# Gates in one narrow pass, and the first norm's gain moved into the weights on GpSimd

## The reference

```python
h = rms_norm(x, norm_mix_g)                 # x * rsqrt(mean(x*x) + eps) * norm_mix_g
proj = jnp.einsum('bsd,de->bse', h, w_in)   # 1024 x 3592
a_q, a_k, a_v, d_qkv, d_z, d_beta, d_alpha = jnp.split(proj, splits, axis=-1)
a_out = chunked_band_attention(a_q, a_k, a_v, ...)      # 8 heads of 64
d_qkv = silu(causal_depthwise_conv(d_qkv, conv_w))
o = gated_delta_rule(d_q, d_k, d_v, d_beta, d_alpha, a_log, dt_bias)   # 4 heads of 128
x = x + concat(norm(a_out), norm(o) * silu(d_z)) @ w_out
x = x + (silu(rms_norm(x, norm_ffn_g) @ w_gate) * (rms_norm(x, norm_ffn_g) @ w_up)) @ w_down
```

## Time and profile before

| | |
|---|---|
| median of three runs | 1297.86 us |
| the profiled execution | 1299.1 us |
| its span in the trace | 1297.4 us |
| PE busy | 1274.9 us (98%) |
| DVE, ACT, POOL busy | 727.2, 581.3, 709.4 us |

### The profile page before, as it was taken

One profiled execution on the slowest core, in us unless ns is written; L12 is line 12 of the kernel. 1 busy time (PEld: TensorE's weight loads), 2 busy tenths in 40 slices (PEclk: granted clock), 3 DMA queues, 4 the chain that ended last, 5 costly groups with the idle time before them and its releaser, 6 DMA issues.

```text
span 1297.4 us, 18370 instructions
## 1 busy us (share of the span) xinstructions
PE 1274.9 (98%) x6956; PEld 1070.5 (83%) x6956; DVE 727.2 (56%) x1034; ACT 581.3 (45%) x931; POOL 709.4 (55%) x486
## 2 busy tenths in 40 slices
PE   8999999999999999999999999999999999999999
PEld 7888888888888877888887888888888888888887
DVE  6455654535716667845486566656555556435552
ACT  5577744654126774552353332233333324644441
POOL 4322455633325572124257996898788784754541
PEclk9999999999999999999999999999999999999999
DMA  5611345531125013553111544432444337986663
GB/s 212 236 58 33 99 136 137 150 114 49 41 45 191 3 30 124 173 187 118 69 66 65 187 187 189 162 148 116 166 187 186 154 122 264 318 287 194 195 194 146
DMA packets 77807, 186.11 MB, mean 143 GB/s; under 512 B 20680, under 2 KB 24848, under 8 KB 70680
## 3 DMA queue, kind: packets, MB, share of 16 engines
q1 hardware_dynamic: 72144, 180.71, 40.6%
q10 hardware_dynamic: 5576, 4.23, 1.1%
HBM read 130.59 MB, written 56.94 MB: 145 GB/s over the span
## 4 chain that ended last, share of the span: by engine, by line
PE 86%; DVE 5%; ACT 3%; POOL 3%; issue 2%; DMA 1%; ACTq 0%; DVEq 0%; POOLq 0%
PE ps L2147 29%; PE ps L364 20%; PE ps L2172 16%; PE ps L377 7%; PE ps L1970 2%; PE ps L2004 2%; PE ps L1992 1%; PE ps L2064 1%; DVE SX L1755 1%; PE ps L1950 1%; PE ps L349 1%; POOL WR L802 1%; PE ps L2022 1%; POOL GR L775 1%; PE ps L2034 1%
## 5 line engine op out<-in xcount | busy, mean ns | idle before, releaser
L364 PE MATMUL ps<-HT,SPLIT 128*128 128x512 f32 (+1 forms) x1488 | 328.4, 378 | 2.5 <-DVE HT L340 2.0
L364 PEld LDWEIGHTS ps<-HT,SPLIT 128*128 128x128 f32 x1488 | 264.5, 188 | 52.5 <-DVE HT L340 2.5
L2172 PE MATMUL ps<-S,HI 128*128 128x512 f32 x616 | 189.6, 389 | 0.0
L978 POOL TENSOR_TENSOR S<-RAB,S 128x512 fp32r<-128x512 f32 x77 | 106.8, 1390 | 93.2 <-ACT S L1149 92.8
L310 POOL CAST SPLIT<-RAW 128x1024 fp32r<-128x1024 f32 x31 | 33.5, 1081 | 187.1 <-PE ps L364 182.2
L2172 PEld LDWEIGHTS ps<-S,HI 128*128 128x128 f32 x616 | 115.7, 188 | 24.1
L2147 PE MATMUL ps<-S,WR 128*128 128x512 f32 x516 | 120.5, 389 | 0.4 <-POOL WR L802 0.4
L2172 PE MATMUL ps<-S,LO 128*128 128x512 f32 x308 | 119.8, 389 | 0.0
L1637 DVE TENSOR_TENSOR LO<-RAB,HI 128x512 fp32r<-128x512 f32 x77 | 66.1, 868 | 92.8 <-ACT HI L1146 92.8
L2147 PE MATMUL ps<-HI,WR 128*128 128x512 f32 x360 | 115.0, 390 | 0.2 <-POOL WR L802 0.2
L2147 PEld LDWEIGHTS ps<-S,WR 128*128 128x128 f32 x516 | 96.8, 188 | 20.8 <-POOL WR L802 0.8
(11 more groups left out here) (278 smaller groups left out, 2489.6 us busy)
## 6 DMA issues: line engine op xcount, KB each, us to landing
hidden<-HB SPq DMA_DIRECT2D x11, 1792.0 KB, 6.6
RAB<-hidden SPq DMA_DIRECT2D x77, 256.0 KB, 3.1
RAW<-units SPq DMA_DIRECT2D x37, 512.0 KB, 4.0
RAWG<-w_gate SPq DMA_DIRECT2D x11, 1024.0 KB, 10.8
RAWU<-w_up SPq DMA_DIRECT2D x11, 1024.0 KB, 4.9
RAWD<-w_down SPq DMA_DIRECT2D x11, 1024.0 KB, 8.8
down_t<-RAWD SPq DMA_DIRECT2D x11, 1024.0 KB, 4.1
RAB<-down_t SPq DMA_DIRECT2D x44, 256.0 KB, 3.4
```

Source lines behind the costliest of these rows:

```text
L364: mm = pe.matmul(ps[:, bank + a // HALF, a % HALF:a % HALF + width], w, right[other][:, k, a:a + width], start=(k == order[0] and part == ...
L978: pool.tensor_tensor(down_b(q, 1), RAB[:, q % RAWS, 1, :], down_b(q, 0).bitcast(F32), ALU.subtract).then_inc(R["b_lo"], 1)
L2172: mm = pe.matmul(ps[:, bank + t, :], down_a(q, part)[:, t * P:(t + 1) * P], down_b(q, other), start=(p == 0 and i in (1, 6, 5, 7) and part ...
```

## The change

- The gate columns come as an array of their own, 64 floats a partition (32 KB), loaded by ACT's queue. `gate_split` on POOL multiplies them by the gain and writes both parts side by side: 16 columns of weights. `gate_columns` on PE makes all four products of parts with 16 matmuls a quarter in place of 24, of 16 output rows. ACT copies 16 rows, and the turn is now a product with `fold`, a 16 x 8 matrix of two unit matrices stacked, which adds the two halves. DVE makes `fold`.
- `units` no longer holds the padded gate unit. SP loads tile 0 behind x block 1, where the gate unit was, and nothing behind block 3.
- The gain is loaded as one column of 8 values a partition, not as 4 KB in every partition. `unit_split` multiplies each of the 28 tiles in `RAW` by it before the cast (a third POOL operation, 128 x 1024). `norm_scale` for this norm is a product with one number a row. Tile 0's split waits until blocks 0 and 1 are scaled.
- 24 transposes at the start in place of 48.
- On DVE: the copy in `EXT` moves behind block 1; `side_split(dve, 0, 0)` moves ahead of the gates' arithmetic; tile 21's copy stands after step 17 of the solve in place of step 20.

```diff
-WARM, WARM_NEXT = 48, 16
+WARM, WARM_NEXT = 24, 16
+NGATE = 2 * NHD
...
         def unit_dma(sp, j, slot):
-            sp.dma_start(RAW[:, slot, :], units[j, :, :]).then_inc(raw_in[slot], 16)
+            sp.dma_start(RAW[:, slot, :], units[j - U_TILE, :, :]).then_inc(raw_in[slot], 16)
...
             pool.wait_ge(raw_in[slot], 16 * turn)
+            if j <= U_OUT:
+                blocks_of = RAW[:, slot, :].rearrange("p (k c) -> p k c", c=P)
+                pool.tensor_tensor(blocks_of, blocks_of, gain_mix_col[:, :].unsqueeze(2).to_broadcast([P, KT, P]),
+                                   ALU.mult).then_inc(hi_done, 1)
+                pool.wait_ge(hi_done, 2 * j - 1)
             ge(pool, unit_used, used)
             pool.tensor_copy(dst[:, 0, :], RAW[:, slot, :]).then_inc(hi_done, 1)
-            pool.wait_ge(hi_done, j)
+            pool.wait_ge(hi_done, j + min(j, U_OUT))
...
+        def gate_split(pool):
+            pool.wait_ge(gain_mix_in, 16)
+            pool.wait_ge(raw_in[0], 16)
+            pool.tensor_tensor(gate_raw, gate_raw, gain_mix_col[:, :].unsqueeze(2).to_broadcast([P, KT, NGATE]),
+                               ALU.mult).then_inc(hi_done, 1)
...
+            if gain_bc is None:
+                dve.tensor_scalar(xn[:, m % 2, :], src, rstd[:, m:m + 1], None, ALU.mult).then_inc(nrm[w]["xn"], 1)
...
+        def gate_columns(pe, bank, right, first, end):
+            for k in range(KT):
+                w = gate_parts[:, k, :, :].rearrange("p a c -> p (a c)")
+                for other in range(2):
+                    mm = pe.matmul(ps[0:2 * NGATE, bank + first // HALF, first % HALF:first % HALF + end - first], w,
+                                   right[other][:, k, first:end], start=(k == 0 and other == 0),
+                                   stop=(k == KT - 1 and other == 1))
...
-                unit_split(pool, 0, 1, 0, 1)
+                gate_split(pool)
+                pool.wait_ge(nrm["inp"]["xn"], 2)
                 unit_split(pool, 1, 1, 0, 2)
...
-                act.dma_start(gain_mix_bc, gain_mix.partition_broadcast(P)).then_inc(gain_mix_in, 16)
+                act.dma_start(gain_mix_col[:, :], gain_mix).then_inc(gain_mix_in, 16)
+                act.dma_start(RAW[:, 0, 0:KT * NGATE], gate_cols).then_inc(raw_in[0], 16)
...
+                side_split(dve, 0, 0)
                 dve.wait_ge(G["act"], 3)
...
-                solve(dve, 8, 20)
+                solve(dve, 8, 17)
                 side_back(dve, SV0 + 1)
-                solve(dve, 20, BLOCK - 1)
+                solve(dve, 17, BLOCK - 1)
...
-                        mm = columns_unit(pe, slot, 4 + 2 * slot, HTP, *span)
+                        if slot == 0:
+                            mm = gate_columns(pe, 4, HTP, *span)
+                        else:
+                            mm = columns_unit(pe, slot, 4 + 2 * slot, HTP, *span)
...
-                    mm = pe.transpose(ps[:, 2, m * 8:(m + 1) * 8], GT[0:8, m * P:(m + 1) * P], ident[0:8, 0:8])
+                    mm = pe.matmul(ps[:, 2, m * NGATE:(m + 1) * NGATE], GT[0:2 * NGATE, m * P:(m + 1) * P], fold[:, :],
+                                   start=True, stop=True)
```

More of the change, by code:

```diff
@@ L180, in hymba_block @@
         gain_att_col = sb("gain_att_col", [P, 4])
+        gain_mix_col = sb("gain_mix_col", [P, KT])
+        fold = sb("fold", [2 * NGATE, NGATE])
         gates = sb("gates", [P, NT, 8])
@@ L263, in hymba_block @@
         XIN = PROJ[:, 20:28, :]
-        gain_mix_bc = PROJ[:, 19, :]
+        gate_raw = RAW[:, 0, 0:KT * NGATE].rearrange("p (k c) -> p k c", c=NGATE)
+        gate_parts = SPLIT[:, 0, 0, 0:2 * KT * NGATE].rearrange("p (k a c) -> p k a c", a=2, c=NGATE)
         XN = PROJ[:, 17:19, :]
@@ L308, in unit_split @@
             pool.wait_ge(raw_in[slot], 16 * turn)
+            if j <= U_OUT:
[3 more added lines that the diff above has]
+                pool.wait_ge(hi_done, 2 * j - 1)
             ge(pool, unit_used, used)
             pool.tensor_copy(dst[:, 0, :], RAW[:, slot, :]).then_inc(hi_done, 1)
-            pool.wait_ge(hi_done, j)
+            pool.wait_ge(hi_done, j + min(j, U_OUT))
             pool.tensor_tensor(dst[:, 1, :], RAW[:, slot, :], dst[:, 0, :].bitcast(F32),
+                               ALU.subtract).then_inc(split_done, 1)
+        def gate_split(pool):
[3 more added lines that the diff above has]
+                               ALU.mult).then_inc(hi_done, 1)
+            pool.wait_ge(hi_done, 1)
+            pool.tensor_copy(gate_parts[:, :, 0, :], gate_raw).then_inc(hi_done, 1)
+            pool.wait_ge(hi_done, 2)
+            pool.tensor_tensor(gate_parts[:, :, 1, :], gate_raw, gate_parts[:, :, 0, :].bitcast(F32),
                                ALU.subtract).then_inc(split_done, 1)
@@ L369, in columns_unit @@
                     mm.then_inc(read, 1)
+            return mm
+        def gate_columns(pe, bank, right, first, end):
[5 more added lines that the diff above has]
+                                   stop=(k == KT - 1 and other == 1))
             return mm
@@ L635, in _ @@
                     if m == 1:
-                        unit_dma(sp, 0, 0)
-                    if m == 3:
                         unit_dma(sp, 1, 1)
@@ L1186, in _ @@
                 act.wait_ge(unit_used, U_GATES + 1)
-                act.activation(GT[0:8].rearrange("p (b c) -> p b c", c=HALF), bank_pair(0, 4)[0:8],
+                act.activation(GT[0:2 * NGATE].rearrange("p (b c) -> p b c", c=HALF), bank_pair(0, 4)[0:2 * NGATE],
                                ACT.Copy).then_inc(banks_free, 1)
@@ L1666, in _ @@
                     dve.sem_inc(one, FREE0)
[L1668 to L1671, removed]
+                dve.wait_ge(consts, 1)
+                dve.tensor_tensor(fold[:, :], ident[0:2 * NGATE, 0:NGATE], ident[0:2 * NGATE, NGATE:2 * NGATE],
+                                  ALU.add).then_inc(J["consts"], 1)
                 for step, m in INP_NORM_DVE:
                     if step == "scale":
-                        norm_scale(dve, "inp", XIN[:, m, :], gain_mix_bc, XN, m)
+                        norm_scale(dve, "inp", XIN[:, m, :], None, XN, m)
+                        if m == 1:
+                            dve.wait_ge(ext_in, 16)
+                            dve.tensor_copy(EXT[0:NHA, 0:4 * P - 1],
+                                            EXT[0:NHA, 4 * P - 1:4 * P].to_broadcast([NHA, 4 * P - 1])).then_inc(ext_filled, 1)
                     else:
@@ L1700, in _ @@
                 dve.tensor_scalar(gq_col[:, :], gq_col[:, :], float(DHA) ** -0.5, None, ALU.mult).then_inc(J["consts"], 1)
-                dve.wait_ge(J["consts"], 3)
-                side_split(dve, 0, 0)
+                dve.wait_ge(J["consts"], 4)
                 for t in range(1, SDV):
@@ L2316, in _units, with _gate_columns @@
 def _units(w_in, w_out):
-    order = [_columns(w_in, j) for j in [NPROJ, *map(row, range(NPROJ))]] + [w_out[j * P:(j + 1) * P, :] for j in range(KT)]
+    order = [_columns(w_in, row(j)) for j in range(NPROJ)] + [w_out[j * P:(j + 1) * P, :] for j in range(KT)]
     return np.ascontiguousarray(np.stack(order))
+def _gate_columns(w_in):
+    c = w_in[:, NPROJ * P:NPROJ * P + NGATE]
+    return np.ascontiguousarray(c.reshape(KT, P, NGATE).transpose(1, 0, 2).reshape(P, KT * NGATE))
 def _column_pairs(w):
@@ L2336 @@
         "x": np.ascontiguousarray(x[0]),
+        "gate_cols": _gate_columns(np.asarray(w_in[0])),
         "units": _units(np.asarray(w_in[0]), np.asarray(w_out[0])),
@@ L2340 @@
         "w_down": _row_pairs(np.asarray(w_down[0])),
-        "gain_mix": np.ascontiguousarray(norm_mix_g[0]),
+        "gain_mix": np.ascontiguousarray(norm_mix_g[0].reshape(KT, P).T),
         "gain_q": np.ascontiguousarray(attn_q_norm_g[0].reshape(DHA, 1)),
```

9 lines of the change are left out of this document (5 added, 4 removed).

## The result

| | before | after |
|---|---|---|
| median (range) | 1297.86 (1296.28 to 1299.87) | 1303.4 (1301.16 to 1304.18) |
| profiled execution, span | 1299.1, 1297.4 | 1303.4, 1301.7 |
| mean granted clock | 0.997 | 0.992 |

The ratio is 1.0038, with a 95% interval of [1.0026, 1.0051]: slower by some 5 us. The 0.3% that the prediction took as its bound lies inside this interval. Executions that took far longer than the rest, here one of 3291 us, are left out everywhere.

A forecast was written before the change was run, and what follows sets the result against it. The prediction took TensorE, holding 86% of the chain, as the bound, with room only in the start. It summed -5.9 - 1.2 + 8.4 + 1.7 = +3.0 us on 1297.9 to 1300.9 us, 8-in-10 range 1291.0 to 1304.5.

The forecast's parts named there:

- the forecast's own range: Whole kernel: 1297 to 1304 us if the forecast's own case, given chance 0.47, holds.
- The start, -5.9: Before the first full tile: PE ends the gates' quarters 5.9 us earlier, 2.9 from loads and warm-up, 3.0 from fewer matmuls.
- side_split, -1.2: Start: tile 0's earlier split removes PE's 1.2 us wait for the parts of its squares.
- The products on POOL: 28 tile products on POOL: 1.89 us each, 53 us in all, none in PE's way.
- my own signs of being wrong: Short DVE operations beside products, PE's longest wait under 4 us, first full tile after 42.7, or a cast late through POOL.
- The solve, +8.4: End of the solve: three products delay DVE 1.55 us each, last operations follow POOL's cast, PE waits 8.4 us for tile 22's copy.
- The clock, +1.7: After PE's long wait: it resumes at half pace for 3.4 us, losing 1.7 us.
- No exclusion by the product: Rival, solve: the product hardly holds DVE's port, no turn is late; -7.1 us, 1290.8; chance 0.20.
- The slipping in ahead of the cast: Rival: products cost DVE 1.2 us each, solve ends before POOL's cast, PE waits 2.6; -3.6 us, 1294.3; chance 0.16.
- The plain price: Rival: POOL products take 2.4 us like the subtraction, PE waits 10.2; +4.8 us, 1302.7; chance 0.17.

The follow-up runs named there:

- copy_at_20: The changed kernel with tile 21's copy back after step 20 of the solve; 1295.44 us, ratio 0.9965 to the kernel before.
- four_left_out: The changed kernel without the POOL product by the gain for tiles 24 to 27; 1291.89 us, ratio 0.9939 to the kernel before.
- copy_at_19: The changed kernel with tile 21's copy after step 19 of the solve in place of 17; 1302.76 us, ratio 1.003 to the kernel before.
- gain_on_act: The changed kernel with the products of tiles 24 to 27 made by ACT in eight pieces each; 1291.08 us, ratio 0.9937 to the kernel before.
- turn_and_add: The changed kernel with the gates' 16 rows turned by 8 transposes and halves added by DVE, not the fold product; 1300.18 us, ratio 1.0008.

## Why the prediction was right

The forecast was 1300.9 by a sum of +3.0; it came to 1303.4, within the forecast's own range, by the mechanism that it named. The likeliest outcome by my chances (0.40) was a change within 0.3%; the ratio of 1.0038 lies above that, with an interval that reaches to both sides of it.

- *The start, -5.9.* The first full tile was to begin at 40.8 and did at 40.05. Up to tile 0's first quarter the gain was 3.7 us (2.9 forecast): block 0 came 1.5 us earlier, the upper bound, and block 2 was ready by 14.7. In the later quarters it was 3.7 (3.0 forecast), since the 1.39 us wait for block 5's low part, which I left standing, became one of 0.62 for a scaling. Against that stands the fold. I priced it as the turn that it replaced, 0.66 us, and it took 1.95. Sum of the parts: -3.7 - 3.7 + 1.3 - 0.4 (the wait for tile 1's parts, gone) = -6.5, against the 6.66 that the start of the tile shows. The 24 transposes took 4.1 us where I had 3.6 by an even price: before, 10 stood in the first 2 us and 21 in the two from 6.9. They ended 0.2 us ahead of block 0, so it cost nothing.
- *What I did not see* is the clock behind the fold. It took 1.6 us back from the start in the profiled execution, and with it start and split ended at -6.4, where I had -7.1.
- *side_split, -1.2*: the wait went, in both kernels that had it moved.
- *The products on POOL.* They took 1.89 to 2.35 us, 1.91 in the middle, and PE never waited for a split. But "POOL is idle 8.3 us before each cast" does not hold throughout: in the kernel before, the casts at 225.46, 240.03 and 254.59 stood 0.43 us behind POOL's work for the delta rule. There the new product runs right up to the cast (218.61 to 220.56, the cast at 220.62), and these casts come 1.5 us late (4.84 us earlier than before, where the one at 204.50 is 6.38 earlier). A late cast was among my own signs of being wrong. It cost nothing here: PE needs a tile's parts only after the tile before, and its waits name no split.
- *The solve, +8.4.* Right in each step: three POOL operations each hold one DVE operation, the last two steps fell behind the cast, tile 22's copy was late, tile 21's was not. The wait is 7.9. In place of four operations left at the cast there were three (345.65, 346.62, 349.03). The runs without these four products have no such wait, and the kernel before has it once it is given the products and the copy at 17. That the Trainium skill's rule (SBUF — State Buffer, section Who interferes with whom) holds for a product whose second input is 8 broadcast values a partition is shown here: 1.90 against 0.32 us. A `tensor_scalar` on DVE, which that section lists as one that may take the shared ports, was held up as well: 2.40 us at 12.27, beside the subtraction of 11.72, where its like took 0.75.
- *The clock, +1.7*: half pace reached over about 4.4 us of resumed work; the distance grew by 2.1 up to the scores at 380.
- *Where the sum fell short.* The clock took 2.0 us more than I had (1.6 near 40, 0.4 behind the wait); the start gave 0.7 more and the wait took 0.5 less. That makes +3.8 in place of +3.0, of the +4.3 between the traces; the other 0.5 is not placed, and the medians lie 5.5 apart. So a part of the nearness is luck: in the start a fold priced 1.3 too low stood against quarters priced 1.5 too low, and the unseen clock against both. No row of before priced that clock, and its cause is open.
- *The rivals.* No exclusion by the product is refuted by the 1.90 us. The slipping in ahead of the cast did not happen in the changed kernel. In copy_at_20 it does, though because the cast comes later and not because a product costs less; its waits of 2.7 us and its 1295.4 are near the 2.6 and 1294.3 worked out for the rival. The plain price was not reached.

One thing the prediction had before it and did not draw: it noted that tile 21's copy left at step 20 would come late, at 341.0, and took the earlier place as harmless. By the same reasoning a late turn of 1.1 us moves the cast, and the cast decides over 8 us.

## What to carry to other kernels

An operation moved to an "idle" GpSimd may be paid by the vector engine's two-input operations beside it: here each product of 1.9 us held one small operation of the solve for as long. Where these form a serial chain ahead of a deadline, give the work to ScalarE or keep it out of that stretch (here 1 us in 40 decided over 8). Before moving a copy earlier because its reader waits a little, ask what else starts when that reader does: here the small wait held back the operation that does the harm. And a price for a small matmul is taken from a row of the same kind: here 8 products with a 16 x 8 matrix took 1.95 us, and 8 transposes of the same rows 0.67.

## What the runs showed of the hardware

- The fold's 8 float32 products of 16 rows by 8 columns stand as 16 instructions and took 1.95 us; 8 transposes of 16 rows took 0.67.
- Three of five profiled executions with fold and the short warm-up (the changed kernel, four_left_out, copy_at_19) show the granted clock at 0.5 for about 3.4 us from about 40 us on, though PE had no idle stretch there; copy_at_20 and gain_on_act, with the same instructions up to that point, don't. The three with transposes or 48 warm-ups don't either. Whether fold and warm-up bring it about is not settled by eight executions; in each of the three the first full tile took 1.6 us longer (12.8 for 11.2).
- The 12 executions of turn_and_add fall into 1296.8 to 1299.3 us, all at a mean clock of 0.996, and 1300.2 to 1303.3, at 0.992 to 0.995. By an estimate one fall of 3.4 us lowers the mean of such a span by 0.0013 (half of 3.4 in 1300), so the groups would be one to three falls apart. No trace shows where these falls lie.
- In the changed kernel the clock fell at 347.3 us, 2 us into the wait, and stood at full again at 357.6, 4.4 us after PE had resumed.
